# One transformer-and-experts network: eight experts as one written-out sequence of weight steps

## The reference, cut to what matters

```python
logits = (xf @ w_router).astype(jnp.float32) + b_router.astype(jnp.float32)
top_val, top_idx = lax.top_k(logits, TOP_K)          # 2 of 8 experts per token
gates = jax.nn.softmax(top_val, axis=-1)
...
# for each expert, on the rows of its tokens:
(silu(x @ w_gate) * (x @ w_up)) @ w_down             # 1024 -> 1408 -> 1024
# rows go back to their tokens, times the gate, and are added to h
```

## Time and profile before

| what | value |
|---|---|
| median of 3 runs | 2454.44 us (2454.4 to 2455.49) |
| span of the profiled execution | 2453.1 us |
| PE, PEld busy | 87%, 82% |
| DVE, ACT, POOL busy | 62%, 43%, 28% |
| bytes moved | 400.66 MB, 163 GB/s over the span |
| first to last `gated` of the experts | 1901.21 to 2432.48 us |

### The profile page before, as it was taken

How to read it: one execution, slowest core, us unless ns; L and a number is a source line. 1 busy time by engine, 2 the same in 40 slices (tenths; PEclk the granted TensorE clock), 3 DMA queues, 4 the chain that set the end, 5 groups by cost and what they waited for, 6 DMA issues and landing times.

```text
span 2453.1 us, 38585 instructions
## 1 busy us (share of the span) xinstructions
PE 2141.2 (87%) x14460; PEld 1999.7 (82%) x14460; DVE 1531.9 (62%) x1964; ACT 1063.4 (43%) x1485; POOL 678.0 (28%) x275
## 2 busy tenths in 40 slices
PE   6999987999999977999867979999876988879797
PEld 6998976999899866999857878998866877868686
DVE  4556956565555575555574355555753886868686
ACT  4344534433443435334432134334442655546464
POOL 2232221222232211222202222222200443434343
PEclk9999989999999988999878779999986999989899
DMA  7554402555455423555410024554412675767574
GB/s 297 191 193 138 172 10 103 172 182 194 159 185 188 155 77 104 172 190 196 145 52 1 1 89 161 187 191 157 168 52 79 254 287 184 287 224 282 197 294 163
DMA packets 73266, 400.66 MB, mean 163 GB/s; under 512 B 8240, under 2 KB 8368, under 8 KB 41136
## 3 DMA queue, kind: packets, MB, share of 16 engines
q1 hardware_dynamic: 72704, 397.22, 46.6%
q10 hardware_dynamic: 432, 1.57, 0.2%
HBM read 397.71 MB, written 1.05 MB: 163 GB/s over the span
## 4 chain that ended last, share of the span: by engine, by line
PE 71%; DVE 17%; issue 5%; ACT 3%; DMA 2%; POOL 0%; DVEq 0%; SPq 0%; ACTq 0%; PEld 0%; PEldq 0%
PE psum L288 20%; PE psum L289 19%; PE psum L290 19%; DVE w_lo L272 6%; DMA ring<-in_stream 2%; PE psum L691 1%; PE psum L699 1%; PE psum L704 1%; PE psum L2128 1%; PE psum L332 1%; ACT w_hi L265 1%; DVE hT_lo L353 1%; ACT O L302 1%; PE psum L2141 1%; DVE act_hi L2405 1%
## 5 line engine op out<-in xcount | busy, mean ns | idle before, releaser
L272 DVE TENSOR_TENSOR w_lo<-ring,w_hi 128x1024 fp32r<-128x1024 f32 x496 | 869.0, 1778 | 427.9 <-ACT w_hi L265 426.8
L278 POOL TENSOR_TENSOR w_lo<-ring,w_hi 128x1024 fp32r<-128x1024 f32 x248 | 630.0, 2540 | 1558.9 <-ACT w_hi L265 1558.9
L265 ACT ACTIVATE w_hi<-ring 128x1024 fp32r<-128x1024 f32 x744 | 736.7, 1049 | 439.7 <-PE psum L290 254.3
L288 PE MATMUL psum<-hT_hi,w_hi 128*128 128x256 f32 x2096 | 590.7, 282 | 24.3 <-DVE hT_lo L353 17.6
L289 PE MATMUL psum<-hT_lo,w_hi 128*128 128x256 f32 x2096 | 589.1, 281 | 0.0
L290 PE MATMUL psum<-hT_hi,w_lo 128*128 128x256 f32 x2096 | 589.1, 281 | 0.0
L288 PE MATMUL psum<-w_hi,hT_hi 128*128 128x256 f32 (+1 forms) x1216 | 395.3, 325 | 59.8 <-issue 27.0
L288 PEld LDWEIGHTS psum<-hT_hi,w_hi 128*128 128x128 f32 x2096 | 399.0, 190 | 30.9 <-issue 24.0
L289 PEld LDWEIGHTS psum<-hT_lo,w_hi 128*128 128x128 f32 x2096 | 399.1, 190 | 3.9
L290 PEld LDWEIGHTS psum<-hT_hi,w_lo 128*128 128x128 f32 x2096 | 398.9, 190 | 0.0
L289 PE MATMUL psum<-w_lo,hT_hi 128*128 128x256 f32 (+1 forms) x1216 | 379.2, 312 | 0.0
(11 more groups left out here) (441 smaller groups left out, 1975.1 us busy)
## 6 DMA issues: line engine op xcount, KB each, us to landing
ring<-in_stream SPq DMA_DIRECT2D x248, 1024.0 KB, 5.3
ring<-in_stream SPq DMA_DIRECT2D x248, 512.0 KB, 4.2
tables<-in_tables SPq DMA_DIRECT2D x1, 2517.0 KB, 20.7
gain_row<-in_gains ACTq DMA_DIRECT2D x3, 512.0 KB, 3.7
rows<-in_rows SPq DMA_DIRECT2D x1, 1288.0 KB, 23.2
X<-in_x SPq DMA_DIRECT2D x1, 1024.0 KB, 4.9
result<-X SPq DMA_DIRECT2D x2, 512.0 KB, 2.7
columns<-in_columns SPq DMA_DIRECT2D x1, 993.0 KB, 15.3
```

The lines of the kernel that those rows point to most:

```text
L265: act.activation(part(w_hi, g, i), ring[:, k, i * PART:(i + 1) * PART], ACT.Copy) \
L272: dve.tensor_tensor(part(w_lo, g, i), ring[:, k, i * PART:(i + 1) * PART], part(w_hi, g, i).bitcast(F32), ALU.subtract) \
L278: pool.tensor_tensor(part(w_lo, g, 2), ring[:, k, 2 * PART:STEP], part(w_hi, g, 2).bitcast(F32), ALU.subtract) \
L288: pe.matmul(out_, w[0], x[0], start=first, stop=False, skip_group_check=True)
```

## The change

The loop over pairs is written out: one sequence of 88 steps `m` = 0 to 87 on each engine, of which `e, s = divmod(m, 11)` is the expert and its step. `jobs(m, tiles)` gives every expert the same side work: in step 0 the result of expert e - 1, in step 1 the pick of e + 1, in steps 1 to 4 the chunks of e - 1, in steps 5 to 10 the pieces of e + 1. The last expert has no pick and no pieces behind it. SP loads the 88 steps as one sequence through the ring (slot = step number modulo 3, for all steps of the program). The numbers that semaphores are waited for are constants now, not registers. Besides, the splits `w_lo` of the first two expert steps on DVE stand ahead of the logits and no longer behind the routing.

```diff
-        def in_ring(g, gv, e=0):
...
+        def in_ring(g, gv):
+
+            return g % SLOTS, gv // SLOTS + 1
...
+        def jobs(m, tiles):
+
+            e, s = divmod(m, EXPERT_STEPS)
+            last, n = e == EXPERTS - 1, len(pieces(tiles))
+            out_ = [(e - 1, "result", 0)] if s == 0 and e > 0 else []
+            out_ += [(e + 1, "pick", 0)] if s == 1 and not last else []
+            out_ += [(e - 1, "chunk", s - 1)] if 1 <= s <= len(CHUNKS) and e > 0 else []
...
+            elif tiles == 1 and s > len(CHUNKS) and not last:
+                out_ += [(e + 1, "piece", p) for p in range(n) if p == s - len(CHUNKS) - 1]
+            return out_
...
+            for m in range(MOE_STEPS):
+                up(m, (0,))
+                if m > 0:
+                    turn(f0 + m - 1)
+                up(m, (1,))
+                if m > 0:
+                    down(m - 1)
+                pe.wait_ge(ffn_up_ready, f0 + m + 1)
+                pe.nop().then_inc(early_used, 1)
+                for x, what, p in jobs(m, tiles):
+                    if what == "piece":
+                        if p == 0 and x >= 2:
+                            pe.wait_ge(chunk_added, len(CHUNKS) * (x - 1))
+                        piece(x, p)
+                    elif what == "chunk":
+                        chunk(x, x % 2, p)
+            turn(f0 + MOE_STEPS - 1)
+            down(MOE_STEPS - 1)
+            for c in range(len(CHUNKS)):
+                chunk(EXPERTS - 1, (EXPERTS - 1) % 2, c)
...
             does(None, dve.tensor_tensor, hn_lo[:, :, :], O[:, :, :], hn_hi[:, :, :].bitcast(F32), ALU.subtract)
+            for g in range(moe_first, moe_first + 2):
+                split_lo(dve, g, g)
             dve.wait_ge(*after("moe logits"))
...
-            for g in range(moe_first, moe_first + 2):
-                split_lo(dve, g, g)
             settle()
             by_load(dve, at, experts_vector)
...
+            for g in range(moe_first, total):
+                load_early(g, g, g - SLOTS)
+                if g > moe_first:
+                    load_late(g - 1, g - 1, g - 1 - SLOTS)
             if moe_first < total:
...
+                load_late(total - 1, total - 1, total - 1 - SLOTS)
```

More of the change, by code:

```diff
@@ L246, in part, with split_hi @@
             return x[:, g % 2, i * PART:(i + 1) * PART]
-        def in_ring(g, gv, e=0):
[L250 to L259, removed]
+        def in_ring(g, gv):
+            return g % SLOTS, gv // SLOTS + 1
+        def split_hi(act, g, gv, parts=range(3)):
+            k, n = in_ring(g, gv)
             for i in parts:
@@ L2039, in pieces @@
             return ["back", "gate"] + [(part_, k) for k in range(0, KT, per) for part_ in range(2)]
[L2041 to L2052, removed]
+        def jobs(m, tiles):
[4 more added lines that the diff above has]
+            out_ += [(e - 1, "chunk", s - 1)] if 1 <= s <= len(CHUNKS) and e > 0 else []
+            if tiles == 2 and s == EXPERT_STEPS - 1 and not last:
+                out_ += [(e + 1, "piece", p) for p in range(n)]
+            elif tiles == 1 and s > len(CHUNKS) and not last:
+                out_ += [(e + 1, "piece", p) for p in range(n) if p == s - len(CHUNKS) - 1]
+            return out_
         def gathered(x, tiles, parity, k):
@@ L2169, in turn, with down @@
                 ins.then_inc(turned_ready, 1)
[L2171 to L2176, removed]
+            def down(m):
+                e, s = divmod(m, EXPERT_STEPS)
+                f, g = f0 + m, moe_first + m
+                pe.wait_ge(lo_last_ready, g + 1)
+                pe.wait_ge(ffn_act_ready, f + 1)
+                if s == 0 and e > 0:
                     pe.wait_ge(y_ready, 2 * tiles * e)
@@ L2183, in down @@
                 ins.then_inc(steps_used, 1)
[L2185 to L2188, removed]
-                up(n, 2 * i + n // EXPERT_STEPS, f, fv, g, gv, (1,))
-                if n > 0:
-                    down(n - 1, 2 * i + (n - 1) // EXPERT_STEPS, f - 1, fv - 1, g - 1, gv - 1)
-                pe.wait_ge(ffn_up_ready, fv + 1)
-                pe.nop().then_inc(early_used, 1)
-                for x, (what, p) in jobs(tiles)[n]:
-                    if what == "piece":
-                        if (x, p) == (2, 0):
-                            pe.wait_ge(chunk_added, len(CHUNKS) * 2 * i + len(CHUNKS))
-                        piece(2 * i + x, p)
-                    elif what == "chunk":
-                        chunk(2 * i + x, x % 2, p)
@@ L2202, in end @@
-            def end(i):
-                n, f0 = PAIR - 1, ffn_steps_before[at]
-                turn(f0 + n, PAIR * i + f0 + n)
-                down(n, 2 * i + 1, f0 + n, PAIR * i + f0 + n, moe_first + n, PAIR * i + moe_first + n)
-                pe.wait_ge(even_taken, half * (2 * i + 2) + half)
-                pe.wait_ge(odd_taken, half * (2 * i + 2) + half)
-                for c in range(len(CHUNKS)):
-                    chunk(2 * i + 1, 1, c)
-                pe.wait_ge(chunk_added, len(CHUNKS) * (2 * i + 2))
@@ L2344, in experts_vector @@
         def experts_vector(dve, at, tiles):
-            slots, n_pieces, half = tiles * P, len(pieces(tiles)), len(pieces(tiles)) // 2
+            slots, n_pieces = tiles * P, len(pieces(tiles))
+            f0 = ffn_steps_before[at]
             def pick(x, first=False):
```

144 lines of the change are left out of this document (57 added, 87 removed).

## The result

The changed kernel takes 2424.49 us (median of 4 runs, 2421.55 to 2424.79) against 2454.42 us before; the ratio is 0.9874 (95% interval 0.9859 to 0.9888). It is faster, as forecast, but by 30 us and not by 64: the time lies outside the range of 2371 to 2404.

What follows compares the result with a forecast made beforehand. DVE and POOL together were taken to bound the plain step, PE close behind. Savings of 54.1 + 7 + 2 + 1 = 64.1 us from 2454.4 gave a forecast of 2390 us, range 2371 to 2404.

Steps and rivals of the forecast that it cites:

- part 1: Between pairs of experts: the drains go and seven experts run at the old odd experts' 60.8 us; 54.1 us saved.
- The prediction's own sign of a wrong mechanism: In the experts: one taking over 61 us with ACT not waiting for the ring, or mid-expert issue stalls on DVE or PE.
- Part 2: Weight loads at expert boundaries: one ring through all 88 steps ends ACT's transfer waits; 7 us saved (0 to 21).
- Rival A: Experts: only the drains go, the port swallows the ring's gain or the odd boundary stays long; 2397 to 2404 us, chance 0.20.
- Part 3: Last expert: no pieces and no pick after expert 7; 2 us saved (0 to 4).
- Part 4: Router: four splits move ahead of the logits; +1 us (-3.3 to +5), the move alone between -3.2 and +1.3.
- B: Rival, experts: deeper relief, seven gain 3 us each if late transfers also stretch chunk steps; 2372 to 2378 us, chance 0.18.
- C: Rival, DVE or PE inside experts: written-out code must be fetched, stalls of 4.6 to 4.9 us each; slower, chance 0.03.
- D: Rival, experts: the parts don't add and the odd cadence isn't reached; time within 0.2%, chance 0.02.
- a clock near 1.00 throughout: Sign for the drains' removal: PE's granted clock in the experts, against 0.68 between pairs before.
- the router's best case: Upper end for the moved splits plus a vanished 4.60 us issue stall in the pick: given as +5 us.

Runs made afterwards that it cites:

- e3_both: Changed kernel with the chunk ahead of the pick in step 1 and the last gathered piece in step 9, not 10: 2388.21 us.
- e5_splitback: Changed kernel with DVE's four splits of the first two expert steps behind the routing again, as before: 2416.39 us.
- e7_fill: Changed kernel with twelve extra matmuls on PE at step 0 of experts 1 to 7, ahead of its wait for the last piece: 2407.74 us.
- f2_pick0: f1 with the pick for expert 1 in step 0 of expert 0, as before, not in step 1: 2382.53 us, ratio to before 0.9703.
- e4_oldring: Changed kernel with the ring's slots of before (step s of each expert in the same slot), 88 steps still written out: 2422.18 us.
- e8_both_oldring: e3_both with the ring's slots of before (step s of each expert in the same slot): 2395.97 us.
- f1: e3_both with DVE's first four splits behind the routing again, as before: 2384.24 us.
- e1_swap: Changed kernel with the chunk of the expert before ahead of the pick on DVE in step 1: 2402.63 us.

## Why the prediction was wrong

**The step that failed is "taken over unchanged" in part 1.** The drains went as told: the three intervals of 27 us are gone, with the stall at the back edge and the table loads. But the cadence of the odd experts of before was carried over as the price of the new order, and the new order differs from it in two places that the text didn't cost. First, the pick stands ahead of the chunk, not behind it. The text that says "because the new order gives every expert the same side work" counted the jobs and didn't look at their order in the step. Second, an odd expert of before also gathers its last piece in step 10, but what came next there was the drain, in which that copy cost nothing. Now the next up product comes at once and waits for it. Each place costs PE an idle time of about 2 us, and behind it the clock falls (the late piece lets it fall at six of seven boundaries).

What that costs a middle expert follows from the traces: 64.9 us against 59.4 in e3_both. Of these 5.4, the two falls of the clock are 3.0 (e5_splitback and e7_fill have the same order without a fall), the piece that is late 1.8 (0.2 in its own interval, 1.6 in the next), and the order of the pick by itself 0.6. In the experts the prediction's working gives 468 us and 501.9 were measured: 4.4 of the 33.7 too many lie in expert 0, where the pick stands in step 1 and not in step 0 (56.0 against 51.6; f2_pick0 takes 52.5), 28.8 in the six middle experts (3.6 in expert 1, 5.1 in each of the others), and 0.5 in the last. Part 1 by itself, without the new ring, is e4_oldring: 506.3 us, where the text gives 477.2. With both places repaired and the old ring (e8_both_oldring), experts 1 to 5 take 60.6 to 60.9 us, where the text has 60.8: the carried price was right for the order that it was read from. The prediction's own sign of a wrong mechanism came up as it says: an expert over 61 us with ACT not waiting for the ring.

**Part 2, the ring.** ACT's waits for the transfer are gone (33.2 us to none), as said. The worth was taken as 1.0 us an expert; e8 against e3 gives 1.2. In the changed kernel as it stands it is 4.4 us for all, with other falls of the clock mixed in. Rival A (the port swallows it all) has fallen.

**Part 3** was taken as 2 us; in e3_both the last expert takes 54.97 us, 4.5 less than a middle one: 1.8 of that in the three intervals from step 1 to 4, where the pick is gone, the rest where the pieces are gone.

**Part 4** was taken as 1 us, and it was 2.3 (36.55 us from `hn_lo` to `gated` before, 34.22 now). The parts of it were wrong in an instructive way. The move itself costs 3.2 to 3.3 us (e5, f1), which was the lower end. What paid for it has nothing to do with it: the stall of 4.60 us between `m_now` and `m_pick` is gone in every written-out version, and ACT's table load of 1.28 us now ends before PE has its product, at 1893.45, where before it stood between the product and the first silu (1899.60). These two less the 3.2 are 2.7 us, near the 2.3. Why the one stall went was not tried; the prediction had put it down to where the code lies, and that is still only argued.

**The rivals.** B, a deeper relief, didn't happen. C, code that has to be fetched as it runs, is refuted for the experts: PE's only wait on issue, 0.8 us, stands at 1895.33, ahead of the first `gated`, and DVE has none behind 1885.50. D was the nearest in kind (results, pieces and picks of every expert meet the loads of every expert), but what kept the odd cadence away was two short waits of PE, for a piece that it gathers last and for a pick that stands behind POOL's split, and the clock behind both. The clock was named among the signs ("a clock near 1.00 throughout") and had no price in the sum. Two bounds of the text are off by about 1 us without a consequence: 2454.4 - 54 - 2 is 2398 for the lower end of A, not 2397, and the router's best case is 1.3 + 4.6 = 5.9, not 5.

## What to carry to other kernels

When a loop is written out and a price is carried over from a stretch of the old trace, compare the order of the instructions in each queue, not the list of jobs, and ask of the last job ahead of a drain who waits for it once the drain is gone. An idle time of 2 us on PE in a dense stretch can cost more than it shows, because the clock may fall behind it (1.5 us here) and the engines behind PE start late in the next step (1.6 us here). A row of the granted clock for each interval tells. Useless matmuls in the wait gave the first back; putting the producer a step earlier gave back both. Work that is moved ahead of a branch no longer covers the stall at the branch.

## What the runs showed of the hardware

The same code with the same idle time of PE ran on with either clock. After 1.92 to 1.95 us of waiting the granted clock of the interval was 1.00 at some boundaries and 0.76 at others, within one run of the changed kernel (one and six of seven), e1_swap (six and one) and e5_splitback (four and three), and the interval 5.6 to 5.7 or 6.9 to 7.2 us. An edit two steps after a boundary (e1) and one ahead of all experts (e5) both changed at which boundaries it falls, so it seems to hang on what PE did earlier; the rule was not settled. The Trainium skill, TensorE: Matmul & The Clock Gate, section "A second HAM failure mode: psum-queue depth-cycling", tells of a clock that swings when PE is idle often and briefly between groups of matmuls; the fall to 0.76 behind 1.92 us agrees, and the six boundaries of e1_swap that kept 1.00 behind 1.92 to 1.95 us show that it need not. A copy of 128x4 elements on DVE took 0.17 us in the router, where POOL doesn't split, and 2.26 to 2.35 us where it began near the start of a POOL split of 2.4 us.
